# Six layer norms in a two-block decoder kernel: who computes their last columns, and in which order the products around them run

## What is computed

```python
for l in range(DEPTH):                       # DEPTH = 2
    h = hybrid_mixer(x, ...)                 # ends in  merged @ w_mix_out
    x = layer_norm(ALPHA * x + h, ln1_g[l], ln1_b[l])
    h = memory_cross_attention(x, mem, ...)  # ends in  o @ x_wo
    x = layer_norm(ALPHA * x + h, ln2_g[l], ln2_b[l])
    h = conv_ffn(x, ...)                     # ends in  z @ f_w_down
    x = layer_norm(ALPHA * x + h, ln3_g[l], ln3_b[l])

def layer_norm(x, g, b):
    mu = mean(x); var = mean((x - mu) ** 2)  # over the 1024 features of a token
    return (x - mu) * rsqrt(var + 1e-5) * g + b
```

## Time and profile before

| | us |
|---|---|
| median of 3 executions | 1663.39 (1661.22 to 1664.31) |
| the profiled execution | 1660.03, of which its span 1658.2 |
| TensorE busy | 1557.0 (94%) |
| VectorE busy | 1028.6 (62%) |
| ScalarE busy | 800.3 (48%) |
| GpSimd busy | 246.6 (15%) |

### The profile page before, as it was taken

How to read it: one execution, slowest core, us unless ns; L and a number is a source line. 1 busy time by engine, 2 the same in 40 slices (tenths; PEclk the granted TensorE clock), 3 DMA queues, 4 the chain that set the end, 5 groups by cost and what they waited for, 6 DMA issues and landing times.

```text
span 1658.2 us, 25362 instructions
## 1 busy us (share of the span) xinstructions
PE 1557.0 (94%) x10403; PEld 1401.7 (85%) x10403; DVE 1028.6 (62%) x1704; ACT 800.3 (48%) x1435; POOL 246.6 (15%) x225
## 2 busy tenths in 40 slices
PE   8999999898998999989989999899988799989999
PEld 6899888798986889988789986697876699979987
DVE  5764585675855575577677865445655486646643
ACT  4545445364642455444356652453445564435532
POOL 2300131211202130032031101003010041100000
PEclk9999999899999999999999999899999899989999
DMA  8523355359554533255345555455211244535543
GB/s 314 222 102 115 103 216 174 119 178 218 190 208 152 203 123 111 88 190 181 128 160 190 182 192 176 152 184 187 90 45 48 77 153 148 202 107 189 188 178 127
DMA packets 41027, 261.33 MB, mean 158 GB/s; under 512 B 4512, under 2 KB 5152, under 8 KB 14672
## 3 DMA queue, kind: packets, MB, share of 16 engines
q1 hardware_dynamic: 35600, 238.44, 41.5%
q0 software_dynamic: 2944, 15.69, 3.7%
q10 hardware_dynamic: 2368, 5.58, 0.9%
HBM read 254.98 MB, written 4.19 MB: 156 GB/s over the span
## 4 chain that ended last, share of the span: by engine, by line
PE 75%; DVE 11%; ACT 5%; issue 3%; DMA 3%; POOL 2%; ACTq 0%; DVEq 0%; POOLq 0%; SPq 0%
PE ps L478 67%; PE ps L581 3%; DMA raw<-d_wst 2%; DVE lows L1503 2%; POOL sm L2189 1%; PE ps L662 1%; ACT wh L998 1%; ACT S L1415 1%; DVE ar L2007 1%; DVE sm L1536 1%; DVE xs L1533 1%; PE ps L683 1%; DVE S L2069 1%; PE ps L577 1%; PE ps L701 0%
## 5 line engine op out<-in xcount | busy, mean ns | idle before, releaser
L1503 DVE TENSOR_TENSOR lows<-raw,wh 128x1024 fp32r<-128x1024 f32 (+3 forms) x473 | 546.1, 1174 | 261.3 <-ACT wh L998 258.5
L478 PE MATMUL ps<-xTr,wh 128*128 128x256 f32 (+2 forms) x3664 | 674.1, 286 | 17.0 <-DVE S L1833 7.5
L478 PEld LDWEIGHTS ps<-xTr,wh 128*128 128x128 f32 (+2 forms) x3664 | 574.7, 192 | 22.3 <-issue 14.2
L998 ACT CAST wh<-raw 128x1024 fp32r<-128x1024 f32 (+3 forms) x473 | 455.6, 989 | 176.1 <-DMA raw<-d_wst 164.4
L478 PE MATMUL ps<-xTr,lows 128*128 128x256 f32 (+2 forms) x1832 | 522.0, 285 | 0.0
L478 PEld LDWEIGHTS ps<-xTr,lows 128*128 128x128 f32 (+2 forms) x1832 | 352.4, 192 | 0.0
L478 PE MATMUL ps<-wh,arR 128*128 128x512 f32 x928 | 296.4, 398 | 4.1 <-DVE ar L1653 4.1
L478 PEld LDWEIGHTS ps<-wh,arR 128*128 128x128 f32 x928 | 175.1, 189 | 48.1 <-DVE ar L1653 5.8
L478 PE MATMUL ps<-lows,arR 128*128 128x512 f32 x464 | 184.1, 397 | 0.0
L478 PE MATMUL ps<-arR,wh 128*128 128x256 f32 (+1 forms) x832 | 147.2, 280 | 2.2 <-DVE lows L1503 2.2
L478 PE MATMUL ps<-wh,xTr 128*128 128x512 f32 x384 | 125.0, 405 | 12.2 <-DVE xTr L1522 6.7
(11 more groups left out here) (265 smaller groups left out, 1554.0 us busy)
## 6 DMA issues: line engine op xcount, KB each, us to landing
raw<-d_wst SPq DMA_DIRECT2D x196, 1024.0 KB, 4.8
raw<-d_wst SPq DMA_DIRECT2D x24, 512.0 KB, 3.5
raw<-d_wst SPq DMA_DIRECT2D x12, 896.0 KB, 4.6
raw<-d_wst SPq DMA_DIRECT2D x8, 672.0 KB, 4.6
ar<-d_lnp POOLq DMA_DIRECT2D x5, 1024.0 KB, 5.2
raw<-d_wst SPq DMA_DIRECT2D x8, 441.0 KB, 3.4
d_scr<-PT POOLq DMA_DIRECT2D x1, 3072.0 KB, 37.0
ar<-d_par POOLq DMA_DIRECT2D x2, 1192.0 KB, 9.6
```

The costliest lines, as they stand in the source:

```text
L478: op = e.matmul(out, s, m, start=start and i == 0, stop=stop and i == len(pairs) - 1)
L998: e.copy(high_of(m), raw_of(m)).then_inc(*high.done(m))
L1503: e.tensor_tensor(low_of(m), raw_of(m), high_of(m).bitcast(F32), ALU.subtract).then_inc(*low.done(m))
```

## The change

It has four parts.

1. All 1024 columns of a layer norm go through VectorE. The constant `H`, ScalarE's `centred` and three of GpSimd's operations for each tile go away, and so does VectorE's negated mean. GpSimd keeps the inverse root (`roots`). The last operation of a tile is done in two column halves of 512, each with its own signal; the turn of a half waits for that half.
2. `down` computes the last four pieces by tile and column half: the first half of tile 0 over all four pieces, then the second half, then tile 1 in the same way. The last four pieces are all released in the last of these four passes.
3. On VectorE, the rounding of tile 0 comes ahead of tile 1's norm in two places: after norm 2 (`normed_second`, between the first residual of tile 1 and its moments) and after norm 3 of layer 0, where the low parts of the next weights are put between the steps of tile 1's norm. ScalarE's casts are put in a matching order.
4. After norm 1 the order on TensorE becomes keys 0, 1, 2, turn of tile 0, turn of tile 1, key 3, with no warming product. ScalarE and VectorE follow; on VectorE the norm of tile 0 comes first, then low parts (of keys 2 and 3, by the look-ahead), then the norm of tile 1.

The diff, cut to its core (the uses of the changed signals and the removed lines of ScalarE and GpSimd described above are left out):

```diff
 # tensor: down
-                kept = []
-                for k in range(kt):
-                    x, (wH, wL) = piece(name, 128, 1, 1024, (key, rw[k:k + 1], span(0, 1024)))
-                    tile(k, x, wH, wL, 0)
-                    if k < kt - tail:
-                        tile(k, x, wH, wL, 1)
-                    else:
-                        kept.append((k, x, wH, wL))
-                for k, x, wH, wL in kept:
-                    tile(k, x, wH, wL, 1)
+                for k in range(kt - tail):
+                    p = rows_of(k)
+                    for i in range(2):
+                        for h in range(2):
+                            part(*p, i, h)
+                    product.also("used", p[1])
+                kept = [rows_of(k) for k in range(kt - tail, kt)]
+                for i in range(2):
                     for h in range(2):
+                        for p in kept:
+                            part(*p, i, h)
+                            if i and h:
+                                product.also("used", p[1])
 # tensor: after norm 1
-                memory_keys(0)
-                memory_keys(1)
+                for j in range(3):
+                    memory_keys(j)
                 stream_turned(tag, 0, xt(0), normed)
-                memory_keys(2)
+                stream_turned(tag, 1, xt(1), normed)
                 memory_keys(3)
-                warm(1)
-                stream_turned(tag, 1, xt(1), normed)
 # scalar: after norm 1
-                centred(tag, 0)
-                centred(tag, 1)
-                memory_keys(0)
-                memory_keys(1)
+                for j in range(3):
+                    memory_keys(j)
                 stream_split(tag, 0, (product, "mix_out", l, 1, 1))
-                memory_keys(2)
+                stream_split(tag, 1, (product, "mix_out", l, 1, 1))
                 memory_keys(3)
-                stream_split(tag, 1, (product, "mix_out", l, 1, 1))
 # scalar: after norm 3 of layer 0
+                    first, *others = pieces.of["kv", l + 1]
+                    highs(first, far=0)
                     stream_split(tag, 0, (product, "up", l, 2 * NZ - 1))
-                    highs_of("kv", l + 1, far=0)
+                    for n in others:
+                        highs(n, far=0)
                     stream_split(tag, 1, (product, "up", l, 2 * NZ - 1))
 # vector: the norm
+            def gained(tag, i):
                 x = xt(i)
                 st, mv, nm, ve_, rs, nr = norm_smalls(i)
...
-                e.scalar_tensor_tensor(x[:, 0:H], x[:, 0:H], mv[:, 0:1], lnp[:, 0:H], ALU.subtract,
+                e.scalar_tensor_tensor(x, x, mv[:, 0:1], lnp[:, 0:1024], ALU.subtract,
                                        ALU.mult).then_inc(*vec.done("gain", *tag, i))
...
+                for h in range(2):
+                    c = slice(512 * h, 512 * h + 512)
+                    e.scalar_tensor_tensor(x[:, c], x[:, c], rs, lnp[:, 1024 + 512 * h:1536 + 512 * h], ALU.mult,
+                                           ALU.add).then_inc(*vec.done("ln", *tag, i, h))
+
+            def normed(tag, name, scale, i):
+                for h in range(2):
+                    residual(tag, name, scale, i, h)
+                    moments(tag, name, i, h)
+                gained(tag, i)
+
+            def normed_second(tag, name, scale):
+                residual(tag, name, scale, 1, 0)
+                stream_split(tag, 0)
+                moments(tag, name, 1, 0)
+                residual(tag, name, scale, 1, 1)
+                moments(tag, name, 1, 1)
+                gained(tag, 1)
 # vector: norm 1
-                centred(tag, ("mix_out", l), 0.5, 0)
-                gained(tag, 0)
-                centred(tag, ("mix_out", l), 0.5, 1)
+                normed(tag, ("mix_out", l), 0.5, 0)
                 lows_for("mk", l, 0)
+                normed(tag, ("mix_out", l), 0.5, 1)
                 lows_for("mk", l, 1)
-                gained(tag, 1)
+                lows_for("mk", l, 2)
                 stream_split(tag, 0)
-                lows_for("mk", l, 2)
+                stream_split(tag, 1)
                 lows_for("mk", l, 3)
-                stream_split(tag, 1)
 # vector: norm 2
-                centred(tag, ("wo", l), 1.0, 0)
-                gained(tag, 0)
-                centred(tag, ("wo", l), 1.0, 1)
-                gained(tag, 1)
-                stream_split(tag, 0)
+                normed(tag, ("wo", l), 1.0, 0)
+                normed_second(tag, ("wo", l), 1.0)
                 stream_split(tag, 1)
 # vector: norm 3
-                centred(tag, ("dn", l), 1.0, 0)
-                gained(tag, 0)
-                centred(tag, ("dn", l), 1.0, 1)
-                gained(tag, 1)
-                if l + 1 < DEPTH:
+                normed(tag, ("dn", l), 1.0, 0)
+                if l + 1 == DEPTH:
+                    normed(tag, ("dn", l), 1.0, 1)
+                else:
+                    first, *others = pieces.of["kv", l + 1]
+                    lows_due(first, far=0)
                     stream_split(tag, 0)
-                    lows_for("kv", l + 1, far=0)
+                    lows_due(others[0], far=0)
+                    for h in range(2):
+                        residual(tag, ("dn", l), 1.0, 1, h)
+                        moments(tag, ("dn", l), 1, h)
+                        lows_due(others[1 + h], far=0)
+                    gained(tag, 1)
                     stream_split(tag, 1)
```

More of the change, by code:

```diff
@@ L546, in down, with part, rows_of @@
                         M.reserve((*name, i, h), vec, "res", *name, i, h)
-                def tile(k, x, wH, wL, i):
-                    c = slice(i * 128, (i + 1) * 128)
+                def part(k, x, wH, wL, i, h):
+                    c, f = slice(i * 128, (i + 1) * 128), slice(h * 512, (h + 1) * 512)
                     w.wait_ge(low, x)
                     w.wait_ge(*ready(k, i))
-                    for h in range(2):
-                        f = slice(h * 512, (h + 1) * 512)
-                        b = M.ready(w, (*name, i, h))
-                        run(b[:, :], three(Y.h[:, k, c], Y.l[:, k, c], wH[:, 0, f], wL[:, 0, f]),
-                            k == 0, k == kt - 1).then_inc(*product.done(*name, i, h))
-                    if i == 1:
-                        product.also("used", x)
-                kept = []
-                for k in range(kt):
-                    x, (wH, wL) = piece(name, 128, 1, 1024, (key, rw[k:k + 1], span(0, 1024)))
-                    tile(k, x, wH, wL, 0)
-                    if k < kt - tail:
-                        tile(k, x, wH, wL, 1)
-                    else:
-                        kept.append((k, x, wH, wL))
-                for k, x, wH, wL in kept:
-                    tile(k, x, wH, wL, 1)
+                    b = M.ready(w, (*name, i, h))
+                    run(b[:, :], three(Y.h[:, k, c], Y.l[:, k, c], wH[:, 0, f], wL[:, 0, f]),
+                        k == 0, k == kt - 1).then_inc(*product.done(*name, i, h))
+                def rows_of(k):
+                    x, (wH, wL) = piece(name, 128, 1, 1024, (key, rw[k:k + 1], span(0, 1024)))
+                    return k, x, wH, wL
+                for k in range(kt - tail):
[6 more added lines that the diff above has]
+                for i in range(2):
+                    for h in range(2):
+                        for p in kept:
+                            part(*p, i, h)
+                            if i and h:
+                                product.also("used", p[1])
             def warm(n):
```

63 lines of the change are left out of this document (19 added, 44 removed).

## The result

The changed kernel takes 1652.02 us (median of four executions, 1650.1 to 1654.48) against 1663.36 for the kernel before in the same session. The two medians differ by 11.3 us; as a ratio with its 95% interval it is 0.9942 (0.9925 to 0.996), or 9.6 us less (6.7 to 12.5). Forecast were 1653.7, range 1649 to 1659.5. The profiled execution took 1651.64, its span 1649.8; before these were 1660.03 and 1658.2.

A forecast was written before the change was run, and what follows sets the result against it. The chain of waits is three quarters TensorE, so only its idle or useless time can be won. Terms -6.9 + 2.5 - 4.4 - 0.9 = -9.7 us, on the median of 1663.39, give 1653.7; range 1649 to 1659.5.

The forecast's parts named there:

- Norm 1: Mixer's projection, two layers: TensorE's waits and warming product go, queries start at 255.8 instead of 259.25, -3.4 us per layer.
- the bound of 3.6: Norm 1: the two waits and the warming product are 3.6 us at most, the limit of the gain per layer.
- The slack: Norm 1: tile 1 is ready 1.8 us before its turn; if it is late, the gain goes.
- Norm 3 of layer 0: End of the feed-forward: tile 1's part of layer 1's keys and values starts at 531.7 instead of 536.17, -4.4 us.
- Norm 3 of layer 1: VectorE no longer waits for ScalarE's squares of tile 0, next step at 1032.7, -0.9 us.
- Norm 2: Output of the cross attention: tile 0's early rounding delays tile 1's norm and turn, +1.4 us in layer 0, +1.1 in layer 1.
- Last products "at nothing": Seven tails that weights follow: pieces held longer, one group per tail reloaded 1.4 us later, costed at nothing, at most 1.4 each.
- the rival of 25 us: Late weights: reloads waited for in all seven tails, half speed following, 25.2 us, total 1679; chance 0.06.
- No gain in norm 1: Rival: if casts wait for a late load, all of the 3.4 us goes in each layer, total 1660.6; chance 0.09.
- a free norm 2: Rival: norm 2 costs nothing, as tile 0's turn and cast come sooner than replayed, total 1651.2; chance 0.1.
- The clock: Rival: TensorE's waits move its 1.2 GHz stretches; two more at 2.2 us each, total 1658.1; chance 0.2.

The follow-up runs named there:

- norm 3 in the old order: The changed kernel with norm 3 of layer 0 ordered as before: both tiles' norms, then tile 0's rounding, then low parts; 1658.75 us, ratio 0.9973.
- late rounding, tile 0 piece by piece: The changed kernel with tile 0 rounded behind tile 1's norm after norm 2, and tile 0 of the cross attention's output computed piece by piece; 1650.9 us, ratio 0.9929.

## Why the prediction was right, and where not

**Norm 1, forecast -3.4 per layer, measured -3.8** to the queries, a little over the bound of 3.6. The order of events was as replayed: the turn starts 28.89 behind the first product, 28.9 by the prediction (250.9 less 222.0). The slack was smaller: tile 1's halves are done at 251.90 and its turn starts at 253.21, 1.3 later, where 1.8 was forecast. That the new order of keys and turns makes 2.7 of it is shown; of the other 1.1 only that it came with parts 1 and 4 together.

**Norm 3 of layer 0, forecast -4.4, measured -4.4** (17.49 to 13.08). The wait for the fourth piece's low parts was put at 0.7 and measured at 0.49. **Norm 3 of layer 1, forecast -0.9, measured -0.9**, and 1.8 more from the clock, which was not forecast.

**Norm 2, forecast +1.4 and +1.1, measured +2.2 and +1.7** up to the next product. This is the mis-sized term. Its step failed at the turn: VectorE's steps came as replayed (variance 5.59 behind the warming product, 5.68 forecast; last operations 7.46, 7.43 forecast), but the turn of half 1 was given some 0.6, and the eight transposes took 1.97 at the lower clock behind a wait that the change itself had lengthened. The next product came 11.73 behind the warming product, 10.98 by the prediction of layer 0. Behind it the two layers part: in layer 0 the lower clock lasted 3.7 us behind that product instead of 5.0, and 0.5 was given back, net +1.6; in layer 1 it lasted 5.0 instead of 3.9, and another 0.5 was lost, net +2.2. Neither bound, that only half of the delay is paid or that half speed lasts as long as before, describes both.

**Last products "at nothing"** was right of the seven tails as to late weights: the rival of 25 us did not come, and the chain's share of loads stayed at 3%. It was wrong of one: where all pieces of a product are last ones, the first half runs through four pieces in the time of two, and the fourth's low parts were 0.78 late in layer 1, where the stretch grew by 1.03 (in layer 0, where part of it ran at 0.50 in both kernels, it grew by 0.04). The prediction looked at who waits for the release of a piece and not at who needs it sooner.

**Sum.** Forecast -9.7; by the ratio -9.6 (interval 6.7 to 12.5), the medians -11.3, the two profiled spans -8.4. Of the spans' sum, norm 1 is -7.7 up to the attention scores (-6.9 forecast), the cross attention's output +1.1 (nothing), norm 2 with what lies behind it +3.8 (+2.5), norm 3 of layer 0 -4.5 (-4.4), norm 3 of layer 1 -0.9 (-0.9) and the stretch behind it -1.8 (nothing). The stretch up to the first projection, which no edit touches, was 1.45 longer: from 90 to 92 us the granted clock was 0.50 in this execution and 0.97 in the one before. So the steps of norms 1 and 3 were right, but that the sum came so near is partly luck: the misses of +1.1 and +1.3 met others of -0.8 and -1.8.

**Rivals.** No gain in norm 1 and a free norm 2 are refuted by the rows above; of late weights behind the tails the chain shows nothing. The clock was half right: it did take its price in norm 2, and it moved single executions by 1.5 to 3 us in stretches that no edit touched, but not in the place named (528 to 532).

## What to carry to other kernels

Before work is moved ahead in an engine's queue, ask what its input waits for: the early rounding won 3.9 us where its turn was ready and lost 2.7 twice where the turn stood behind all products. A wait that grows on TensorE can cost more than its length: the eight transposes behind it took 1.97 instead of 1.13 in layer 0, and 1.97 instead of 1.69 in layer 1. Reordering a product so that one half ends sooner also makes it need its last piece sooner; both ends of the order must be looked at. A part of a change is priced alone only if nothing of the other parts stays with it: here the low parts of the keys stayed at their new place when the columns were to be shown alone.

## What was not expected of the hardware

**GpSimd is held for a whole operation of VectorE.** An inverse root on 128 x 1 values takes 0.55 alone, 1.38 to 1.40 beside VectorE's operation on 832 columns with two SBUF inputs, 1.52 to 1.54 on 1024 and 0.98 to 1.01 on 512, and ends about 0.4 behind the end of that operation. "SBUF — State Buffer" in the Trainium skill, SBUF: two separate sides, describes this as an exclusive lock for a whole instruction between a VectorE instruction with two SBUF inputs and a GpSimd one that reads SBUF; the rows agree. The operation that the prediction lengthened at no cost, since it ends before the root, is itself what makes the root long: from the variance to the last operation it is 1.86 instead of 1.72.

**TensorE's clock differs where the instructions are the same.** In the first products of a projection it fell to 0.50 in some profiles and stayed at 1.00 in others, though order and waits there are the same (45.69 or 47.24, behind a wait of 1.38): 1.55 each time. The two layers of one execution differ in the same way (45.69 and 47.23 with norm 3 in the old order). The executions of one kernel (late rounding, tile 0 piece by piece) spread from 1645.3 at a mean clock of 0.976 to 1651.5 at 0.971. Differences below 3 us between two medians are therefore told here by stretches, not by the totals alone.
